# One-hot rows and gate pieces from per-token compares with per-partition scalars, in the gate stage of a PEER layer

## The chip, the core and the metric

The kernel runs on one core of a Trainium2 chip. The metric is the device time of one execution in microseconds (us), taken as the median of several runs. Engines are named as in the profile: PE (TensorE's matmuls) and PEld (its weight loads), DVE (VectorE), ACT (ScalarE), POOL (GpSimd), SP (SyncE, which issues the DMAs here).

## What is computed

One layer of a streaming encoder over 512 prompt tokens and 32 sample tokens (544 in all) with model width 1024: differential attention and retention, cross attention, and then a PEER layer, which is where the change lies. The PEER part of the reference, cut:

```python
q = (hb @ w_pq).reshape(PEER_BLOCK, PEER_HEADS, 2, D_KEY // 2)
s1 = einsum('tpd,pnd->tpn', q[:, :, 0], pk1); s2 = einsum('tpd,pnd->tpn', q[:, :, 1], pk2)
v1, i1 = lax.top_k(s1, 16); v2, i2 = lax.top_k(s2, 16)
cand = v1[..., :, None] + v2[..., None, :]
sc, pos = lax.top_k(cand.reshape(..., 256), 16)
e = take_along_axis(i1[..., :, None] * 128 + i2[..., None, :], pos)
gate = softmax(sc)
act = gelu(einsum('tpkd,td->tpk', u_tab[e], hb))
out = einsum('tpk,tpkd->td', gate * act, v_tab[e])
```

There are 8 heads, 128 keys on each side, 128 x 128 = 16384 experts and 16 chosen experts per head, so each token has 128 chosen (key 1, key 2, gate) triples.

## The kernel before, in words

The kernel gathers nothing. It computes the activation of every expert for every token (128 blocks of `u`, each of 128 experts by 1024, times the 1024 x 544 hidden state), builds a dense gate for every expert and token, multiplies the two, and multiplies the result with all of `v`.

Products in f32 quality are made of three passes with operands split into a high and a low half (`passes`, lines 725 to 730). For each block of `u`, SP loads it into a ring (`weights`, L363), ACT makes the high half (`high`, L1443), POOL makes the low half (`low`, L640: block minus high half, one operation of 128 x 1024 with two inputs in SBUF), PE runs `unit` for the two halves of the tokens (8 chunks x 3 passes x 2 = 48 matmuls of 272 columns, L728 to L730), ACT applies Gelu (L1476) into `actb`, and SP stores it to scratch (L556). Two slots of high and low halves alternate.

The dense gates come from one-hot rows. The 128 chosen triples of a token lie on the 128 partitions: `selT[:, 0]` holds key 1, `selT[:, 1]` key 2, `selT[:, 2]` the gate, each with one column per token. For a token, `hot2` is the row of 128 columns that is 1 where the column number equals key 2; `gated` is the row that holds the gate where the column number equals key 1, and 0 elsewhere. A matmul of the two sums over the 128 triples and gives the token's 128 x 128 gates. To keep f32 quality with bf16 operands, the gate is split into three bf16 `pieces`, so there are three `gated` rows per token and three matmuls into the same output.

The work is grouped by 8 tokens (`TOK8`), 4 such groups (`GROUP`) to a chunk of 32 tokens, 17 chunks (`NCHUNK`): 68 groups in all. Order on each engine in this stage, which is written out by hand:

- PE (L1127 to L1130): for each group one `first_products` unit (48 matmuls, 128 blocks of `u` in all, 68 of them in this stage) and then `gate_products` (L1116 to L1125): wait for `hot_ready`, then 8 tokens x 3 pieces = 24 matmuls of 128 columns in bf16 (L1123) into two banks of 4 tokens each, with `g_ready` raised after each bank. Before the stage PE runs units alone, and after it 8 more units (`U3_GROUPS`), and then the second products with `v`.
- ACT (`gate_chunk`, L1503 to L1514): the next block's high half, two Gelus, and two copies of the gates (L1512) from the banks into `gst`.
- SP: the block loads and activation stores, and once per chunk the store of `gst` (L562).
- POOL: one low half per unit.
- DVE (L1870 to L1890): once, the three pieces of all gates (L1872, L1874); then for each group, after a wait for `g_ready` that lets it run two groups ahead of PE (`hot2` and `gated` have two slots each, `j % 2`): a wide compare that makes `hot1` for 8 tokens (L1885), a semaphore step, a wide compare that makes `hot2` (L1886), and three wide multiplies of `hot1` by a piece (L1888). Each has 8 x 128 = 1024 columns; the per-token values are spread over 128 columns with a step of 0. The last raises `hot_ready`.

DVE has no other work in this stage. `iota` holds 0 to 127 in every partition, in f32.

Of the kernel before, what the change touches and what calls it, by code (L numbers as in the profile page):

```python
# [26 lines left out]
ALU = mybir.AluOpType  # L27
# [4 lines left out]
BF16 = mybir.dt.bfloat16  # L32
U32 = mybir.dt.uint32

P = 128
# [6 lines left out]
NT = len(TILES)  # L42
# [6 lines left out]
KEYS = 128  # L49
# [46 lines left out]
TOK8 = 8  # L96
CTOK = GROUP * TOK8
# [38 lines left out]
def encoder_step(nc, d):  # L136

    with ExitStack() as whole:
# [14 lines left out]
        iota = plan.place("iota", [P, P])  # L153
# [105 lines left out]
        gates_at = first.end  # L259
        gate_plan = Plan(nc, gates_at)  # L260
        hot2 = gate_plan.place("hot2", [P, 2, TOK8, KEYS], BF16)
        hot1 = gate_plan.place("hot1", [P, 2, TOK8, KEYS], BF16)
        gated = gate_plan.place("gated", [P, 2, 3, TOK8, KEYS], BF16)
        pieces = gate_plan.place("pieces", [P, 3, NT * P], BF16)
        selT = gate_plan.place("selT", [P, 3, NT * P])
        gst = gate_plan.place("gst", [P, 2, KEYS, CTOK])
        sel = gate_plan.place("sel", [P, NT, 3, P])
# [1297 lines left out]
        def _(dve):  # L1565
            step = Steps(dve, vec)
# [53 lines left out]
            for m in range(2):  # L1620
                a = dve.tensor_tensor_reduce(out=lam_in[:, 2 * m], in0=lam_in[:, 2 * m], in1=lam_in[:, 2 * m + 1],
                                             scale=1.0, scalar=0.0, op0=ALU.mult, op1=ALU.add,
                                             accum_out=lam[:, m:m + 1])
# [180 lines left out]
            for x in (v16, i16, c16, p16):  # L1804
                a = step.link(dve.memset(x[:], 0))
# [62 lines left out]


            dve.wait_ge(selT_taken, 1)  # L1870
            for q in range(3):
                step.link(dve.tensor_copy(pieces[:, q], selT[:, 2]))  # L1872
                if q < 2:
                    step.link(dve.tensor_tensor(selT[:, 2], selT[:, 2], pieces[:, q], ALU.subtract))  # L1874
            with dve.Fori(0, NCHUNK) as i:
                step.restart()
                for j in range(GROUP):
                    dve.wait_ge(g_ready, (i * GROUP + j) * 2 + 2)
                    tok = bass.ds(i * CTOK + j * TOK8, TOK8)

                    def spread(k):
                        return selT[:, k, tok][:, :, None].to_broadcast([P, TOK8, KEYS])

                    every = iota[:][:, None, :].to_broadcast([P, TOK8, KEYS])
                    step.link(dve.tensor_tensor(hot1[:, j % 2], every, spread(0), ALU.is_equal))  # L1885
                    dve.tensor_tensor(hot2[:, j % 2], every, spread(1), ALU.is_equal)  # L1886
                    for q in range(3):
                        a = dve.tensor_tensor(gated[:, j % 2, q], hot1[:, j % 2],  # L1888
                                              pieces[:, q, tok][:, :, None].to_broadcast([P, TOK8, KEYS]), ALU.mult)
                    a.then_inc(hot_ready, 1)  # L1890


# [136 lines left out]
```

## Time and profile before

| | |
|---|---|
| median of 3 runs | 2628.68 us (2627.41 to 2629.49) |
| span of the profiled execution, first to last instruction | 2627.8 us |
| PE busy in the span | 2351.1 us (89%) |
| DVE busy | 1824.0 us (69%) |
| ACT busy | 868.8 us (33%) |
| POOL busy | 900.5 us (34%) |
| first and last group of gate products on PE start at | 1096.7 and 1635.2 us |
| mean granted TensorE clock, share of full speed | 0.960 |

For the profiled execution the profile gives the span; the runs' own times are from 0.4 us below it to 1.7 us above it, with the median 0.9 us above it. A line of the profile names the source line, the engine, the operation, output and inputs by the program's names, the shape (partitions x columns and type), the number of instructions, busy time and mean time of one, and the idle time of the engine just before them with what ended it. Names are without their numbers, so `hot1` and `hot2` both read `hot`. A tile written without an input shape has input and output of one shape. In the timeline the first two columns are start and duration in us, and neighbouring instructions of one kind are merged into one line with their count.

### The profile page before, as it was taken

Reading aid. Unit: us, or ns where it says so; the run is one execution under the profiler, and the core shown is the slowest. Engines: PE = TensorE matmul, PEld = TensorE weight load, DVE = VectorE, ACT = ScalarE, POOL = GpSimd, SP = SyncE. Lnnn points to the kernel's source line nnn. Section 1 sums busy time; section 2 is a strip of 40 time slices with the busy share of each in tenths; the row PEclk is TensorE's granted clock in tenths of the full one; section 3 lists DMA queues with packets and bytes.
Section 4 is the critical chain, followed back from the end, with each engine's and each line's share of the span. In section 5 each row is a group of like instructions: output and inputs, shape, how many; then the busy total and the mean of one; then the engine's idle time right before and its main releaser. Section 6 shows DMA issues by size and latency. Waiting matters only on the chain.

```text
span 2627.8 us, 49280 instructions
## 1 busy us (share of the span) xinstructions
PE 2351.1 (89%) x18541; PEld 2281.4 (87%) x18541; DVE 1824.0 (69%) x2736; ACT 868.8 (33%) x1375; POOL 900.5 (34%) x352
## 2 busy tenths in 40 slices
PE   5999987887999995999999999999889989998997
PEld 5888877787899995999999999988888888888887
DVE  6344454346888898699999998166666666666665
ACT  4434333232234432344444444322212221222121
POOL 2212232133233342333333333534433433343331
PEclk9999998998999997999999999999999999999998
DMA  4232121211223442344444444664454455444530
GB/s 184 83 101 99 58 78 67 78 48 56 80 95 132 133 135 73 123 164 163 162 162 168 167 166 170 225 213 140 152 166 136 142 155 164 132 148 154 159 98 34
DMA packets 168557, 339.18 MB, mean 129 GB/s; under 512 B 10512, under 2 KB 84400, under 8 KB 166192
## 3 DMA queue, kind: packets, MB, share of 16 engines
q1 hardware_dynamic: 168496, 338.46, 38.7%
q8 instruction: 27, 0.44, 0.1%
q14 instruction: 34, 0.28, 0.0%
HBM read 260.04 MB, written 78.38 MB: 129 GB/s over the span
## 4 chain that ended last, share of the span: by engine, by line
issue 35%; PE 35%; POOL 12%; DVE 11%; ACT 6%; DVEq 0%; POOLq 0%; DMA 0%; ACTq 0%; SPq 0%
POOL u_lo L640 11%; PE bank L728 10%; PE bank L730 9%; PE bank L729 9%; DVE w_lo L1896 6%; ACT v_hi L1525 3%; ACT w_hi L1530 1%; PE bank L790 1%; DVE wf L1907 1%; PE bank L997 1%; DVE mixedT L1599 1%; PE bank L781 1%; PE bank L1025 1%; DVE rmo L1721 1%; DVE xT L1917 1%
## 5 line engine op out<-in xcount | busy, mean ns | idle before, releaser
L728 PE MATMUL bank<-h_hi,u_hi 128*128 128x272 f32 x3136 | 926.0, 295 | 83.0 <-POOL u_lo L640 32.6
L730 PE MATMUL bank<-h_hi,u_lo 128*128 128x272 f32 x3136 | 913.8, 291 | 0.0
L729 PE MATMUL bank<-h_lo,u_hi 128*128 128x272 f32 x3136 | 909.7, 290 | 0.0
L640 POOL TENSOR_TENSOR u_lo<-wring,u_hi 128x1024 fp32r<-128x1024 f32 x196 | 521.8, 2662 | 1067.9 <-ACT u_hi L1443 667.7
L728 PE MATMUL bank<-w_hi,v_hi 128*128 128x272 f32 x2048 | 613.6, 300 | 101.6 <-DVE xT L1917 98.4
L728 PEld LDWEIGHTS bank<-h_hi,u_hi 128*128 128x128 f32 x3136 | 598.6, 191 | 95.8 <-issue 63.3
L729 PE MATMUL bank<-w_lo,v_hi 128*128 128x272 f32 x2048 | 609.7, 298 | 0.0
L730 PE MATMUL bank<-w_hi,v_lo 128*128 128x272 f32 x2048 | 607.9, 297 | 0.0
L729 PEld LDWEIGHTS bank<-h_lo,u_hi 128*128 128x128 f32 x3136 | 598.8, 191 | 0.5
L730 PEld LDWEIGHTS bank<-h_hi,u_lo 128*128 128x128 f32 x3136 | 597.1, 190 | 0.0
L640 POOL TENSOR_TENSOR v_lo<-wring,v_hi 128x1024 fp32r<-128x1024 f32 x128 | 346.8, 2739 | 542.3 <-ACT v_hi L1525 542.3
L728 PEld LDWEIGHTS bank<-w_hi,v_hi 128*128 128x128 f32 x2048 | 407.0, 199 | 108.4 <-DVE xT L1917 105.0
L729 PEld LDWEIGHTS bank<-w_lo,v_hi 128*128 128x128 f32 x2048 | 405.9, 198 | 0.0
L730 PEld LDWEIGHTS bank<-w_hi,v_lo 128*128 128x128 f32 x2048 | 405.5, 198 | 0.0
L1917 DVE TENSOR_TENSOR xT<-bank,xT 128x272 f32<-128x272 f32 x512 | 204.4, 437 | 281.6 <-PE bank L730 281.4
L1888 DVE TENSOR_TENSOR gated<-hot,pieces 128x1024 bf16<-128x1024 bf16 x204 | 377.9, 1907 | 0.0
L1525 ACT ACTIVATE v_hi<-wring 128x1024 fp32r<-128x1024 f32 x128 | 125.4, 1048 | 448.8 <-PE bank L730 437.8
L1896 DVE TENSOR_TENSOR w_lo<-wf,w_hi 128x544 fp32r<-128x544 f32 x128 | 211.4, 1651 | 59.3 <-ACT w_hi L1530 56.4
L1476 ACT ACTIVATE actb<-bank 128x272 f32<-128x272 f32 x256 | 101.9, 399 | 449.8 <-PE bank L730 447.7
L1907 DVE TENSOR_TENSOR wf<-a,g 128x544 f32<-128x544 f32 x128 | 184.5, 1462 | 34.2 <-DMA g<-scratch_gates 29.6
L1530 ACT ACTIVATE w_hi<-wf 128x544 fp32r<-128x544 f32 x128 | 80.3, 650 | 244.1 <-DVE wf L1907 244.1
L1512 ACT ACTIVATE gst<-bank 128x512 f32<-128x512 f32 x136 | 139.5, 1137 | 60.2 <-PE bank L1123 60.2
(223 smaller groups left out, 1988.0 us busy)
## 6 DMA issues: line engine op xcount, KB each, us to landing
wring<-in_u SPq DMA_DIRECT2D x128, 512.0 KB, 3.7
wring<-in_v SPq DMA_DIRECT2D x128, 512.0 KB, 3.3
scratch_act<-actb SPq DMA_DIRECT2D x128, 272.0 KB, 2.1
scratch_gates<-gst SPq DMA_DIRECT2D x17, 2048.0 KB, 7.3
a<-scratch_act SPq DMA_DIRECT2D x32, 1088.0 KB, 7.2
g<-scratch_gates SPq DMA_DIRECT2D x32, 1088.0 KB, 9.9
wring<-in_w_in SPq DMA_DIRECT2D x28, 512.0 KB, 3.8
wring<-in_w_x SPq DMA_DIRECT2D x24, 512.0 KB, 4.1
```

Source lines behind the costliest of these rows:

```text
L640: pool.tensor_tensor(dst, wring[:, slot], hi.bitcast(F32), ALU.subtract).then_inc(lo_ready, 1)
L728: pe.matmul(out, whi, xhi, start=first, stop=False)
L729: pe.matmul(out, whi, xlo, start=False, stop=False)
L730: return pe.matmul(out, wlo, xhi, start=False, stop=last)
L1476: act.activation(actb[:, j, half(h)], bank[(2 * j + h) % 4][:, 0:HT], ACT.Gelu).then_inc(unit_taken, 1)
L1512: act.activation(gst[:, p, :, t0:t0 + 4].rearrange("p k t -> p t k"), bank[4 + b][:].rearrange("p (t k) -> p t k", t=4), ACT.Copy).then_in ...
L1525: act.activation(vs[p][0][:, j].rearrange("p (c n) -> p c n", c=C), wring[:, j], ACT.Copy).then_inc(hi_ready, 1)
L1530: act.activation(wbs[p][0][:, j], wf[:, j % 2], ACT.Copy).then_inc(whi_ready, 1)
L1888: a = dve.tensor_tensor(gated[:, j % 2, q], hot1[:, j % 2], pieces[:, q, tok][:, :, None].to_broadcast([P, TOK8, KEYS]), ALU.mult)
L1896: dve.tensor_tensor(wbs[p][1][:, j], wf[:, j % 2], wbs[p][0][:, j].bitcast(F32), ALU.subtract).then_inc(w_ready, 1)
L1907: dve.tensor_tensor(wf[:, j % 2].rearrange("p (c t) -> p c t", c=NCHUNK), aring[p][:, j].rearrange("p (c t) -> p c t", c=NCHUNK), gring[p] ...
L1917: dve.tensor_tensor(xT[:, b, half(h)], bank[n % 8][:, 0:HT], xT[:, b, half(h)], ALU.add).then_inc(y_taken, 1)
```

## The change

`hot1` goes away. Each token gets four operations of 128 columns: one compare of the key numbers `keys_h` (bf16) with the token's key 2, read from a column of `selT` as a per-partition scalar, and three operations that compare with key 1 and multiply by a piece of the gate, both per-partition scalars. Both scalars of an operation have one type, so `pieces` is now kept in f32: each is rounded to bf16 in `rounded` and cast back. `keys_h` is made once from `iota`. The waits and the semaphore for PE stay as they are; the semaphore step between `hot1` and its readers goes.

```diff
@@ -259,9 +259,10 @@
         hot2 = gate_plan.place("hot2", [P, 2, TOK8, KEYS], BF16)
-        hot1 = gate_plan.place("hot1", [P, 2, TOK8, KEYS], BF16)
+        keys_h = gate_plan.place("keys_h", [P, KEYS], BF16)
         gated = gate_plan.place("gated", [P, 2, 3, TOK8, KEYS], BF16)
-        pieces = gate_plan.place("pieces", [P, 3, NT * P], BF16)
+        rounded = gate_plan.place("rounded", [P, NT * P], BF16)
+        pieces = gate_plan.place("pieces", [P, 3, NT * P])
@@ -1868,25 +1869,22 @@
             dve.wait_ge(selT_taken, 1)
+            step.link(dve.tensor_copy(keys_h[:], iota[:]))
             for q in range(3):
-                step.link(dve.tensor_copy(pieces[:, q], selT[:, 2]))
+                step.link(dve.tensor_copy(rounded[:], selT[:, 2]))
+                step.link(dve.tensor_copy(pieces[:, q], rounded[:]))
                 if q < 2:
                     step.link(dve.tensor_tensor(selT[:, 2], selT[:, 2], pieces[:, q], ALU.subtract))
             with dve.Fori(0, NCHUNK) as i:
                 step.restart()
                 for j in range(GROUP):
                     dve.wait_ge(g_ready, (i * GROUP + j) * 2 + 2)
-                    tok = bass.ds(i * CTOK + j * TOK8, TOK8)
-
-                    def spread(k):
-                        return selT[:, k, tok][:, :, None].to_broadcast([P, TOK8, KEYS])
-
-                    every = iota[:][:, None, :].to_broadcast([P, TOK8, KEYS])
-                    step.link(dve.tensor_tensor(hot1[:, j % 2], every, spread(0), ALU.is_equal))
-                    dve.tensor_tensor(hot2[:, j % 2], every, spread(1), ALU.is_equal)
-                    for q in range(3):
-                        a = dve.tensor_tensor(gated[:, j % 2, q], hot1[:, j % 2],
-                                              pieces[:, q, tok][:, :, None].to_broadcast([P, TOK8, KEYS]), ALU.mult)
+                    for u in range(TOK8):
+                        tok = bass.ds(i * CTOK + (j * TOK8 + u), 1)
+                        dve.tensor_scalar(hot2[:, j % 2, u], keys_h[:], selT[:, 1, tok], None, ALU.is_equal)
+                        for q in range(3):
+                            a = dve.tensor_scalar(gated[:, j % 2, q, u], keys_h[:], selT[:, 0, tok],
+                                                  pieces[:, q, tok], ALU.is_equal, ALU.mult)
                     a.then_inc(hot_ready, 1)
```

## Rows read from the trace of the kernel before

**Rows 1.** The page's part 2: busy tenths and granted clock in 40 slices.
```profile
DVE  6344454346888898699999998166666666666665
...
PEclk9999998998999997999999999999999999999998
```

**Rows 2.** Busy time of a stretch: window, length, then PE, PEld, DVE, ACT, POOL, clock, DMA.
```profile
1200.00:1300.00 100.00, 93.87 (x887) 91.32 (x886) 98.29 (x63) 46.03 (x63) 37.67 (x13) 1.00 0.45 162
```

**Rows 3.** Groups of instructions, 1165 to 1643 us: busy us, mean ns, idle before.
```profile
L1888 DVE TENSOR_TENSOR gated<-hot,pieces 128x1024 bf16<-128x1024 bf16 x174 | 329.8, 1951 | 0.0
...
L640 POOL TENSOR_TENSOR u_lo<-wring,u_hi 128x1024 fp32r<-128x1024 f32 x59 | 177.7, 3012 | 300.0 <-ACT u_hi L1443 300.0
...
L1123 PE MATMUL bank<-gated,hot 128*128 128x128 bf16 x1416 | 89.2, 219 | 30.2 <-DVE gated L1888 30.2
...
L1886 DVE TENSOR_TENSOR hot<-iota,selT 128x1024 bf16<-128x1024 f32 x58 | 71.1, 1225 | 8.3
L1885 DVE TENSOR_TENSOR hot<-iota,selT 128x1024 bf16<-128x1024 f32 x58 | 70.3, 1212 | 0.0
```

**Rows 4.** Timeline of PE: starts of the gate products.
```profile
1096.72 1.51 PE L1123 MATMUL bank<-gated,hot 128*128 128x128 bf16 x24
...
1148.85 1.51 PE L1123 MATMUL bank<-gated,hot 128*128 128x128 bf16 x24
...
1205.49 1.51 PE L1123 MATMUL bank<-gated,hot 128*128 128x128 bf16 x24 [0.51 <-DVE gated L1888]
...
1213.60 1.51 PE L1123 MATMUL bank<-gated,hot 128*128 128x128 bf16 x24 [0.51 <-DVE gated L1888]
...
1635.23 1.51 PE L1123 MATMUL bank<-gated,hot 128*128 128x128 bf16 x24 [0.51 <-DVE gated L1888]
```

**Rows 5.** Timeline of DVE: the third group's first operation; one whole group; the next one's first.
```profile
1098.38 1.23 DVE L1885 TENSOR_TENSOR hot<-iota,selT 128x1024 bf16<-128x1024 f32 x1 [5.42 <-PE bank L1123]
...
1205.29 1.21 DVE L1885 TENSOR_TENSOR hot<-iota,selT 128x1024 bf16<-128x1024 f32 x1
1206.64 1.23 DVE L1886 TENSOR_TENSOR hot<-iota,selT 128x1024 bf16<-128x1024 f32 x1
1207.79 5.68 DVE L1888 TENSOR_TENSOR gated<-hot,pieces 128x1024 bf16<-128x1024 bf16 x3
1213.39 1.21 DVE L1885 TENSOR_TENSOR hot<-iota,selT 128x1024 bf16<-128x1024 f32 x1
```

**Rows 6.** Timeline of POOL.
```profile
1073.44 2.39 POOL L640 TENSOR_TENSOR u_lo<-wring,u_hi 128x1024 fp32r<-128x1024 f32 x1 [1.09 <-ACT u_hi L1443]
...
1209.34 3.04 POOL L640 TENSOR_TENSOR u_lo<-wring,u_hi 128x1024 fp32r<-128x1024 f32 x1 [5.06 <-ACT u_hi L1443]
```

**Rows 7.** DVE groups of one shape each, whole span.
```profile
L1664 DVE TENSOR_SCALAR ri<-ri,lam 128x1 f32<-128x1 f32 x16 | 3.4, 214 | 0.6
...
L1762 DVE TENSOR_SCALAR xn<-xm 128x1 f32<-128x1 f32 x16 | 2.5, 154 | 0.5
...
L1666 DVE TENSOR_SCALAR S<-S,ri 128x512 f32<-128x512 f32 x4 | 1.9, 487 | 0.1
...
L1666 DVE TENSOR_SCALAR S<-S,ri 128x128 f32<-128x128 f32 x4 | 1.1, 287 | 0.1
```

**Rows 8.** Timeline of DVE: eight pointer operations, and short copies between register operations.
```profile
2619.06 5.66 DVE L1581 SCALAR_TENSOR_TENSOR yT<-xT,gains,rms 128x544 f32<-128x544 f32 x8
...
669.01 0.23 DVE L1837 COPY pos<-p 128x80 uint32 x1
669.15 0.23 DVE L1838 CAST key<-i 128x80 uint32 x1
```

**Rows 9.** One source line's instructions: durations min, median, max in ns.
```profile
L1888 DVEq FUSED_REGOPS  x204: 53/53/64, 1078.1 to 1628.6; - x102
```

**Rows 10.** Timeline of DVE: the first gate pieces.
```profile
1068.76 0.49 DVE L1872 CAST pieces<-selT 128x640 bf16<-128x640 f32 x1 [20.39 <-ACT selT L1497]
...
1070.15 2.56 DVE L1872 CAST pieces<-selT 128x640 bf16<-128x640 f32 x1
```

## Prediction

> **What bounds the kernel now.** Read the page's slices first. From the eighteenth to the twenty-fourth slice DVE stands at nine tenths, which it holds for more than one slice nowhere else, with TensorE's clock granted at nine tenths or more [rows 1]; that is the stage in which unit products and gate products alternate, and the only one the change touches. In a stretch of it DVE is busy 98.3 of 100 us, PE 93.9, ACT 46.0, POOL 37.7 [rows 2]. The grouped instructions then say who waits: 59 groups of gate products lie in the window and PE idles 30.2 us ahead of them, ended by the last `gated` product, while DVE's operations have next to no idle time [rows 3]. The timeline gives both paces. Before DVE binds, the gate products start at 1096.72 and, seven intervals later, at 1148.85: 7.45 us apart, PE's own pace with all its work. Later they start at 1205.49 and 1213.60: 8.11 us, with 0.51 us of waiting shown [rows 4]. Of 68 groups 60 are at DVE's pace, from 1096.72 to 1635.23. So the stage can shrink to 67 x 7.45 = 499.2 us from 538.5 us: **39.3 us is all that a faster DVE can give**.
>
> DVE's 8.11 us divide so: the first compare starts at 1205.29, the second at 1206.64, the three multiplies at 1207.79, the next group at 1213.39 [rows 5]. An independent operation starts about 0.08 us before the one ahead ends (1.23 long, 1.15 to the next). Five operations without a stall make 1.35 + 1.15 + 3 x 1.14 = 5.92 us; the other 2.2 us is a stall, one per group, laid on one `gated` product (mean 1951 ns in the groups, three together 5.68 [rows 3, 5]). Its cause stands on POOL: its `u_lo` takes 2.39 us where DVE has almost let go, and 3.04 us here, from 1209.34 to 1212.38 [rows 6], the span of the stretched DVE operation. They take turns for something both read through; POOL comes once per group, before and after.
>
> **The change, part by part.** *Removed:* five operations of 1024 columns, 5.92 us a group. *Added:* 8 tokens x 4 = 32 operations of 128 columns, one with one pointer scalar and three with two. No row shows such an operation, so I build it. A TENSOR_SCALAR with a pointer on 512 columns takes 487 ns, on 128 columns 287 ns: 0.52 ns a column (two columns a cycle, f32) and 220 ns fixed [rows 7]. Eight pointer operations in a row confirm the overlap: 5.66 us, first-to-last spacing 0.70 for one of 0.78 [rows 8]. So spacing is duration less 0.08. In bf16 on both sides I take half that time per column: 33 ns, duration 253, **spacing 173 ns**. Bounds: below, the short copies, which start 0.14 us apart with 42 ns of columns [rows 8], so 0.135; above, one column a cycle as in the wide compares (1.21 us for 1024, [rows 5]), 133 ns instead of 33, so 0.273.
>
> The **second pointer** has no row. One costs 214 - 154 = 60 ns on one column [rows 7]. The second may be fetched right behind the first (0) or after it (60 ns). I take 0, since a fetch of one column that costs 60 ns is nearly all latency, and two latencies can overlap; it is a choice, and the largest unknown: 24 x 60 = 1.44 us a group.
>
> Register operations grow from about one per wide operation, 53 to 64 ns [rows 9], to one or two per small one, on DVE's sequencer. The copies keep 0.14 us apart with one each; two would make some 0.19, 24 times: 5.5 us a group, which the 2.2 us stall lets run ahead. I cost them at nothing (cover: the operations' own spacing); uncovered, 0.02 x 24 = 0.5 us a group.
>
> *POOL's stall* stays at 2.2 us if the small operations use that shared path, and goes if they don't. POOL's own operation gets shorter (it waits for 0.2 us of DVE work, not up to 1.2). The Trainium skill ("SBUF — State Buffer", Who interferes with whom) says that a copy or tensor_scalar in a two-port mode and GpSimd lock each other out for a whole instruction; the trace agrees for the cast that took 0.49 us alone and 2.56 us beside POOL [rows 10].
>
> Sum in DVE's time: 32 x 0.173 + 2.20 = **7.74 us a group** against 8.11. DVE can run only two groups ahead, so its chain starts at the third group, 1098.38 [rows 5], and has 66 groups: 66 x 0.37 = 24.4 us less; the end of the gates moves from 1635.2 to 1610.8, above PE's own floor of 1596.
>
> The Trainium skill ("VectorE: DVE Perf Modes", The TRN2 errata) speaks against the change: a fixed latency per instruction, to be spread over tiles of 512 elements or more. Its table has 58 cycles plus columns over four, an estimate of 94 ns each; by it the group would be 3.0 + 2.2 us and PE would set the pace. The rows here have a dearer fixed part, with the pointer in it.
>
> *Preparation, once:* one cast of `iota`, three casts back to f32 (0.49 us each by the unblocked cast, [rows 10]), at worst two more POOL stalls of 2.1: 2 to 6 us. DVE is idle 5.42 us ahead of the third group [rows 5] and is two groups ahead of PE then, so nothing lands on the path; without that cover, up to 6 us once. The moved buffers add no transfer; SP and POOL issue the same work. What follows the gates (last unit products, then the second products) is PE's and only starts earlier. Next late after DVE is PE; ACT has half its time free, and `u_lo` ends at 1212.38, 2.5 us before its products could start (1213.60 + 1.32), so POOL has room at 7.45 us too.
>
> The span is 2627.8 us, the median of the runs 2628.7: 0.9 us above. 2628.7 - 24.4 = **2604 us**.
>
> **Rivals.**
> *A. PE's floor.* If the small operations come out at 0.16 us or less (the copies say 0.135 to 0.15), DVE needs 32 x 0.16 + 2.2 = 7.3 us and PE's 7.45 us rules: 2628.7 - 39.3 = 2589 us. For: the copies. Against: they have no pointer.
> *B. The second pointer is paid in full (slower).* Place: the 24 two-pointer operations of each group. 8 x 0.173 + 24 x 0.233 + 2.2 = 9.18 us; 66 x 1.07 = 70.6 us more: 2699 us. It decides from (8.11 - 7.74) / 24 = 15 ns per second pointer on. For: one pointer is visibly not hidden. Against: nothing but the overlap argument.
> *C. The faster column rate is not taken*, so the change doesn't do what it says: 32 x 0.273 = 8.74 us. At one column a cycle it reads through one path alone, so the stall goes too; 66 x 0.63: 2670 us. At two columns a cycle (0.207) with the stall it would be 8.82 us, 2676 us. For: no row has bf16 in and out of a TENSOR_SCALAR. Against: the f32 rows reach two columns a cycle with a pointer.
> *D. POOL can't get in between closely following small operations* and waits for all 32: its `u_lo` would end some 3 us later in the period, about at the point where the product needs it; DVE then has no stall, and the pace is about the same 7.7 us. It changes no number, so it shares the forecast's chance.
>
> **How the numbers follow.** Forecast (with D) 0.38, A 0.15, B 0.26, C 0.12; the remaining 0.09 is a second pointer that costs part, around 10 to 20 ns, which lands within a few us of no change on either side. A difference under about 0.2% (5 us) can't be told from none. Faster: 0.38 + 0.15 and a little of the rest, 0.54; same 0.07; slower 0.26 + 0.12 and a little, 0.39. The range goes from just under A to B: 2587 to 2700. Both signs hold much chance; the forecast's own range, with the spacing between 0.16 and 0.18, is 2589 to 2618.
>
> **What would show it.** The gate products' interval: 7.74 us right, 7.45 A, 9.2 B, 8.7 C. The spacing of one-pointer against two-pointer operations: 173 and 173, or 173 and 233. Their duration: 253 ns, or 353 in C. The stall: one small operation in each group stretched by 2.2 us where POOL works; `u_lo` near 2.4 us instead of 3.0. PE's wait for `gated` in most groups, but about 0.2 us instead of 0.5. The forecast is wrong if the gate stage doesn't carry the whole difference.

## The result and the profile after

| | before | after |
|---|---|---|
| median, us | 2629.1 | 2685.2 |
| ratio to before | | 1.0216, interval 1.0202 to 1.0231 |
| span of the profiled execution, us | 2627.8 | 2684.4 |
| first to last group of gate products, us | 538.5 | 586.1 |
| interval of the gate products where DVE binds, us | 8.11 | 8.81 |
| mean granted TensorE clock | 0.960 | 0.958 |

The change makes the kernel **56.1 us slower**; the forecast was 25 us faster. The number lies inside the range, near rival B (2699 us). The spans differ by 56.6 us: 47.6 in the gate stage, 2.0 ahead of its first product (1098.72 against 1096.72) and 7.0 behind it (985.8 us from the start of the last group of gate products to the start of the kernel's last matmul, 978.8 before). The 2.0 us are there before the changed part runs: DVE's first instruction of it starts, with the same idle time ahead of it, at 1070.81, in the kernel before at 1068.76 [rows 10].

```profile
1070.81 0.23 DVE L1872 CAST keys_h<-iota 128x128 bf16<-128x128 f32 x1 [20.38 <-ACT selT L1498]
```

The page's part 2 of the kernel after, in slices of 67 us. The stretch of nines on DVE is longer and fuller than in [rows 1]; the clock is as high as before.

```profile
DVE  5444454347888896999999999266666666566665
...
PEclk9999998899999997999999999999998999999998
```

A window in the middle of the stage, columns as in [rows 2]: DVE is busy all 100 us instead of 98.3, PE falls from 93.9 to 86.6, POOL from 37.7 to 26.8.

```profile
1200.00:1300.00 100.00, 86.57 (x830) 84.23 (x829) 100.00 (x368) 42.88 (x58) 26.82 (x11) 1.00 0.39 138
```

The timeline of PE, for [rows 4]. The first group of gate products waits for nothing. In mid stage they start 8.82 us apart (8.81 is the usual interval, and 64 of 67 are near it; the other three are 7.45), and the wait ahead of them has gone from 0.51 to 1.2 us. 64 x 8.812 + 3 x 7.447 = 586.3 us, the stage.

```profile
1098.72 1.51 PE L1124 MATMUL bank<-gated,hot 128*128 128x128 bf16 x24
...
1199.85 1.51 PE L1124 MATMUL bank<-gated,hot 128*128 128x128 bf16 x24 [1.19 <-DVE gated L1886]
...
1208.67 1.51 PE L1124 MATMUL bank<-gated,hot 128*128 128x128 bf16 x24 [1.22 <-DVE gated L1886]
...
1684.82 1.51 PE L1124 MATMUL bank<-gated,hot 128*128 128x128 bf16 x24 [1.21 <-DVE gated L1886]
```

The timeline of DVE where POOL's turn falls, for [rows 5]. A token without a stall runs from 1202.98 to 1203.81: 0.16 us to the first multiply, 0.67 us for the three of them. The next `hot2` takes 2.39 us instead of 0.24.

```profile
1202.98 0.24 DVE L1884 TENSOR_SCALAR hot<-keys_h,selT 128x128 bf16<-128x128 bf16 x1
1203.14 0.74 DVE L1886 TENSOR_SCALAR gated<-keys_h,selT,pieces 128x128 bf16<-128x128 bf16 x3
1203.81 2.39 DVE L1884 TENSOR_SCALAR hot<-keys_h,selT 128x128 bf16<-128x128 bf16 x1
1206.12 0.75 DVE L1886 TENSOR_SCALAR gated<-keys_h,selT,pieces 128x128 bf16<-128x128 bf16 x3
```

The timeline of POOL, for [rows 6]: its low half begins 0.10 us ahead of that stalled operation and takes 2.44 us instead of 3.04.

```profile
1203.71 2.44 POOL L641 TENSOR_TENSOR u_lo<-wring,u_hi 128x1024 fp32r<-128x1024 f32 x1 [6.38 <-ACT u_hi L1444]
```

The instructions of the two lines, shortest, median and longest in ns, with the register operations of DVE's sequencer. One pointer takes 244 ns, two take 303 (the stalled ones are the longest). Each compare has one register operation of 57 ns; of the gated ones (three to a token) two in three have one, and there is an address operation of 40 ns per token.

```profile
L1884 DVEq FUSED_REGOPS  x544: 57/57/75, 1080.5 to 1679.2; - x182
L1884 DVE TENSOR_SCALAR hot<-keys_h,selT x544: 235/244/2448, 1080.7 to 1683.8; 128x128 bf16<-128x128 bf16 x182
...
L1886 DVE TENSOR_SCALAR gated<-keys_h,selT,pieces x1632: 296/303/2553, 1080.8 to 1684.4; 128x128 bf16<-128x128 bf16 x182
L1886 DVEq FUSED_REGOPS  x1088: 57/57/75, 1080.7 to 1679.8; - x182
L1886 DVEq ALU_OP  x544: 40/40/40, 1080.8 to 1679.6; - x182
```

The groups from 1165 to 1690 us, for [rows 3]. The stall now sits on `hot` (mean 514 ns over operations of 244), and 59 groups of gate products wait 72.0 us in all, 1.22 us each, where it was 0.51.

```profile
L1886 DVE TENSOR_SCALAR gated<-keys_h,selT,pieces 128x128 bf16<-128x128 bf16 x1415 | 353.7, 303 | 0.0
...
L1884 DVE TENSOR_SCALAR hot<-keys_h,selT 128x128 bf16<-128x128 bf16 x471 | 241.9, 514 | 0.0
...
L1124 PE MATMUL bank<-gated,hot 128*128 128x128 bf16 x1436 | 90.4, 219 | 72.0 <-DVE gated L1886 72.0
```

The spacings are 0.163 us behind a compare and 0.223 us behind a gated operation. So DVE's group is 8 x 0.163 + 24 x 0.223 = 6.66 us of operations, against 5.92 before, and 8.81 less that leaves 2.15 us for POOL's stall, against 2.2. The small operations alone lose 0.74 us a group, and the stall gives back almost nothing of it.

### The profile page after: what moved, and what is told of

Read it like the earlier page. It is cut to its first block, busy times and chain, and to the rows that moved or that the text cites. A ratio compares the mean times of both kernels' runs of the same rounds, so it can differ in the third digit from the quotient of the medians.

```text
span 2684.4 us, 52956 instructions
## 1 busy us (share of the span) xinstructions
PE 2358.4 (88%) x18541; PEld 2287.6 (85%) x18541; DVE 1887.2 (70%) x4576; ACT 867.9 (32%) x1375; POOL 861.3 (32%) x352
## 4 chain that ended last, share of the span: by engine, by line
issue 37%; PE 35%; POOL 11%; DVE 11%; ACT 6%; DVEq 0%; POOLq 0%; DMA 0%; ACTq 0%; SPq 0%
POOL u_lo L641 10%; PE bank L729 10%; PE bank L731 9%; PE bank L730 9%; DVE w_lo L1894 6%; ACT v_hi L1526 3%; ACT w_hi L1531 1%; PE bank L791 1%; DVE wf L1905 1%; DVE mixedT L1600 1%; PE bank L998 1%; PE bank L782 1%; PE bank L1026 1%; DVE rmo L1722 1%; DVE xT L1915 1%
## 5 line engine op out<-in xcount | busy, mean ns | idle before, releaser
L641 POOL TENSOR_TENSOR u_lo<-wring,u_hi 128x1024 fp32r<-128x1024 f32 x196 | 481.0, 2454 | 1157.7 <-ACT u_hi L1444 756.1
L1886 DVE TENSOR_SCALAR gated<-keys_h,selT,pieces 128x128 bf16<-128x128 bf16 x1632 | 420.9, 311 | 0.0
L1884 DVE TENSOR_SCALAR hot<-keys_h,selT 128x128 bf16<-128x128 bf16 x544 | 270.4, 497 | 0.5 <-DVE pieces L1875 0.5
```

Source lines behind the costliest of these rows:

```text
L641: pool.tensor_tensor(dst, wring[:, slot], hi.bitcast(F32), ALU.subtract).then_inc(lo_ready, 1)
L1884: dve.tensor_scalar(hot2[:, j % 2, u], keys_h[:], selT[:, 1, tok], None, ALU.is_equal)
L1886: a = dve.tensor_scalar(gated[:, j % 2, q, u], keys_h[:], selT[:, 0, tok], pieces[:, q, tok], ALU.is_equal, ALU.mult)
```

## The experiments

**The second pointer by itself.** In the gated operation the second scalar becomes a constant; its length in columns, its output and POOL's work stay. The gates are then made without their values (each is the same constant), so the PEER outputs are not the reference's.

```diff
-                            pieces[:, q, tok], ALU.is_equal, ALU.mult)
+                            0.0625, ALU.is_equal, ALU.mult)
```

> The 24 gated operations of a group keep their compare, their multiply and their first pointer scalar; the second scalar is the constant 0.0625 (so the gates are not the reference's). If each pointer scalar is fetched after the one before it (about 59 ns each, from 303 against 244 ns in the changed kernel), the gated operations fall to 244 ns and 0.165 us apart, the group to 32 x 0.165 + 2.14 = 7.4 us, and PE's own 7.45 us rules: 67 x 7.45 = 499 us of gate stage against 586, about 2598 us in all. If the second arithmetic step costs the 59 ns, nothing changes: 8.81 us a group, 2685 us.

Measured: 2600.3 us, 0.9888 of before (0.9872 to 0.9905). The stage takes 498.9 us and the gate products start 7.45 us apart. The source line of the gated operation, then the timeline of one token and the two ahead of and behind it:

```profile
L1886 DVE TENSOR_SCALAR gated<-keys_h,selT x1632: 235/246/2490, 1079.5 to 1590.3; 128x128 bf16<-128x128 bf16 x182
```

```profile
1201.98 0.24 DVE L1884 TENSOR_SCALAR hot<-keys_h,selT 128x128 bf16<-128x128 bf16 x1
1202.14 0.57 DVE L1886 TENSOR_SCALAR gated<-keys_h,selT 128x128 bf16<-128x128 bf16 x3
1202.63 0.24 DVE L1884 TENSOR_SCALAR hot<-keys_h,selT 128x128 bf16<-128x128 bf16 x1
```

With one pointer a gated operation takes the compare's 246 ns, and a token takes 0.65 us instead of 0.83. The group's sum is 8 x 0.65 + 2.2 = 7.4 us, at PE's pace, and PE shows no wait for DVE any more. **The second pointer costs 59 ns of an operation's duration and 60 of the spacing (0.223 against 0.163), and it alone turns the change from a gain of 29 us to a loss of 56.**

**DVE's sequencer.** Another way to 59 ns more per operation is the register work that the moving token index brings, which e1 lessens too. Here both pointers stay and the index is fixed, so that no register operations are left in the loop; every chunk of tokens then takes the first chunk's keys and gates, so the gates are not the reference's.

```diff
-                        tok = bass.ds(i * CTOK + (j * TOK8 + u), 1)
+                        tok = slice(j * TOK8 + u, j * TOK8 + u + 1)
```

> All pointer scalars of the changed kernel point to columns that are fixed per group of the loop body, so no register arithmetic stands ahead of any operation (the gates are those of the first 32 tokens again and again, so not the reference's). If the sequencer's register operations set the pace, the 32 operations come closer together and the group falls well under 8.81 us (towards 7.45). If the pointer fetch in the operation sets it, durations stay 244 and 303 ns, the group stays at 8.81 us and the time at 2685 us.

Measured: 2688.1 us, 1.0222 (1.0205 to 1.0239); interval 8.81, operations of 246 and 305 ns. Nothing is gained, so the register work is hidden and the 59 ns go with the second pointer scalar in the operation itself.

**The column rate.** `iota` is read in f32 in place of its bf16 copy, in both operations (the compare's edit is shown, the gated operation has the same).

```diff
-                        dve.tensor_scalar(hot2[:, j % 2, u], keys_h[:], selT[:, 1, tok], None, ALU.is_equal)
+                        dve.tensor_scalar(hot2[:, j % 2, u], iota[:], selT[:, 1, tok], None, ALU.is_equal)
```

> The 32 operations read the f32 iota in place of the bf16 keys_h. If the changed kernel's operations take four columns a cycle and these take two, each gets 33 ns longer (277 and 336 ns), the group goes to 8.81 + 1.07 = 9.9 us and the time to about 2685 + 66 x 1.07 = 2756 us. If the bf16 operations did not take the fastest rate, nothing changes: 2685 us.

Measured: 2761.9 us, 1.0509 (1.0491 to 1.0526); interval 9.92. Timeline of DVE, one token:

```profile
1200.57 0.28 DVE L1884 TENSOR_SCALAR hot<-iota,selT 128x128 bf16<-128x128 f32 x1
1200.77 0.84 DVE L1886 TENSOR_SCALAR gated<-iota,selT,pieces 128x128 bf16<-128x128 f32 x3
```

The medians are 275 and 336 ns, 31 and 33 more. At two columns a cycle 128 columns take 67 ns ([rows 7]), at four 33: the difference is what going from the one to the other gives, so the changed kernel does run at the faster rate. Rival C, with 353 ns an operation, is out by the 244 ns already. 32 x 0.033 = 1.06 us of the 1.11 us a group are accounted for.

**Where the buffers lie.** The change also moves the stage's buffers, which could be behind the 7 us at the end. The kernel before with a gap of 1280 bytes ahead of `selT`, which puts `selT` and what lies behind it where the change puts them (`gated` and `pieces` stay):

```diff
+        gate_plan.place("gap", [P, 640], BF16)
```

> The kernel before with 1280 bytes left free ahead of selT, so that the buffers behind lie where the change puts them; no instruction differs. The changed kernel is 7 us slower also behind the gate stage. If the moved buffers cause that, this one is at about 2629 + 7 = 2636 us. If they don't, it is at 2629 us.

Measured: 2629.4 us, 1.0000 (0.9991 to 1.0010), 978.6 us from the start of the last group of gate products on. Moving these buffers does nothing.

**A version that keeps the wide operations and takes the bf16 rate.** Two tokens lie innermost (pair, column, token of the pair), keys and index are copied to bf16 once, so every operand of the five wide operations is bf16 and advances by neighbouring elements; PE reads its operands at every second element.

```diff
-        hot2 = gate_plan.place("hot2", [P, 2, TOK8, KEYS], BF16)
+        hot2 = gate_plan.place("hot2", [P, 2, TOK8 // R, KEYS, R], BF16)
...
+        keys_r = gate_plan.place("keys_r", [P, KEYS, R], BF16)
+        keys_t = gate_plan.place("keys_t", [P, 2, T], BF16)
...
-                            m = pe.matmul(bank[4 + b][:, k * P:(k + 1) * P], hot2[:, j % 2, 4 * b + k],
-                                          gated[:, j % 2, q, 4 * b + k], start=q == 0, stop=q == 2)
+                            r, o = (4 * b + k) // R, (4 * b + k) % R
+                            m = pe.matmul(bank[4 + b][:, k * P:(k + 1) * P], hot2[:, j % 2, r, :, o],
+                                          gated[:, j % 2, q, r, :, o], start=q == 0, stop=q == 2)
...
-                        return selT[:, k, tok][:, :, None].to_broadcast([P, TOK8, KEYS])
+                        return x.rearrange("p (a r) -> p a r", r=R)[:, :, None, :].to_broadcast(whole)
```

> From the kernel before: the five wide operations of a group are kept, but all operands are bf16 and the tokens lie in pairs innermost (4 pairs x 128 columns x 2 tokens), so that no operand repeats one element along the innermost dimension. PE reads its gate operands with a step of 2 elements. If the wide compare and multiply then take two columns a cycle: 0.61 us apart, 5 x 0.61 + 0.15 + 2.2 = 5.4 us a group, PE's 7.45 us rules and the time is about 2629 - 39 = 2590 us. If they stay at one column a cycle, 2629 us or a little more. If PE reads strided operands at half the rate, the gate products take 1.3 us more per group: 8.8 us, about 2675 us.

Measured with R = 2: **2592.2 us, 0.9862 (0.9845 to 0.9878)**, the fastest of all that ran, and it beats both kernels. Groups of its stage (1165 to 1560 us):

```profile
L1895 DVE TENSOR_TENSOR gated<-hot,pieces 128x1024 bf16<-128x1024 bf16 x159 | 216.3, 1415 | 0.0
...
L1893 DVE TENSOR_TENSOR hot<-keys_r,keys_t 128x1024 bf16<-128x1024 bf16 x53 | 36.7, 692 | 7.5
L1892 DVE TENSOR_TENSOR hot<-keys_r,keys_t 128x1024 bf16<-128x1024 bf16 x53 | 36.7, 692 | 103.8 <-PE bank L1127 103.8
```

A wide compare takes 692 ns instead of 1212, without a pointer. The multiplies, whose operands are bf16 in both kernels, go from a median of 1219 ns to 685; the longest, 3420 and 2884, hold the stall, which is still on one of the three. The source lines of the multiplies, the kernel before first:

```profile
L1888 DVE TENSOR_TENSOR gated<-hot,pieces x204: 1208/1219/3420, 1079.2 to 1631.7; 128x1024 bf16<-128x1024 bf16 x102
```

```profile
L1895 DVE TENSOR_TENSOR gated<-hot,pieces x204: 682/685/2884, 1078.4 to 1586.5; 128x1024 bf16<-128x1024 bf16 x102
```

DVE now waits for PE, 1.96 us a group. The Trainium skill ("VectorE: DVE Perf Modes", What auto-detection actually checks) says that an operation with two tensor inputs gets its doubled rate where every tensor is 16-bit with a step of one element; the trace agrees: 1219 ns for a multiply with the values spread at step 0 along the innermost dimension, 685 with pairs there. PE has become the bound, as its timeline shows with no wait ahead of the gate products:

```profile
1200.47 1.55 PE L1127 MATMUL bank<-gated,hot 128*128 128x128 bf16 x24
1207.95 1.55 PE L1127 MATMUL bank<-gated,hot 128*128 128x128 bf16 x24
```

7.48 us apart, 0.03 above the floor of 7.45, which is about what the gate products grew by (1.55 for 1.51).

**All eight tokens innermost.** The same with R = 8: fewer dimensions for DVE, and PE reads at every eighth element, 16 bytes apart.

> As v1_pairs with all eight tokens innermost (128 columns x 8 tokens), so PE reads with a step of 8 elements (16 bytes). If the rate of the wide operations depends only on two neighbouring elements, it is as v1_pairs on DVE; if PE's reading depends on the step, it shows here and not there: gate products above 1.5 us a group. 2590 us if neither costs.

Measured: 3012.5 us, 1.1465 (1.1445 to 1.1484). DVE's operations are the same 692 ns. Group and timeline of PE:

```profile
L1127 PE MATMUL bank<-gated,hot 128*128 128x128 bf16 x694 | 168.2, 415 | 0.0
```

```profile
1203.98 5.81 PE L1127 MATMUL bank<-gated,hot 128*128 128x128 bf16 x24
```

The 24 gate products take 5.81 us instead of 1.51, and each group 13.65 us. That is more than the 4.3 us that they grew by (7.45 + 4.3 = 11.8). The remaining 1.9 us are the clock's. The mean granted clock of the stage falls to 0.76, where v1 has 1.00 in the same window:

```profile
1200.00:1300.00 100.00, 100.00 (x538) 85.38 (x537) 39.31 (x37) 27.63 (x37) 17.72 (x8) 0.76 0.28 96
```

PE is busy all 100 us here; the level falls to 1.2 GHz during the slow gate products and rises some 4.5 us after them. The unit products ahead of a group and behind it show the two levels:

```profile
1203.72 0.29 PE L732 MATMUL bank<-h_lo,u_hi 128*128 128x272 f32 x1
1203.85 0.29 PE L733 MATMUL bank<-h_hi,u_lo 128*128 128x272 f32 x1
...
1209.81 0.43 PE L732 MATMUL bank<-h_lo,u_hi 128*128 128x272 f32 x1
1210.04 0.43 PE L733 MATMUL bank<-h_hi,u_lo 128*128 128x272 f32 x1
```

Some 19 unit products behind each group start 0.23 us apart instead of 0.125, which makes 2.0 us. The gate products themselves are 0.23 us apart at either level, so their slowness is not the clock's. The Trainium skill ("SBUF — State Buffer", Specifications (TRN2)) gives lines of 16 bytes and asks for two hits in each for full bandwidth: a step of 16 bytes has one hit per line, a step of 4 bytes has four, and 5.81 against 1.55 us goes with that. Both operands of the matmul have the step; no run tells which of them costs the time.

**The 7 us behind the stage.** They came with `after` (985.8 us from the start of the last group of gate products to the start of the last matmul), e1 (989.7), e2 (989.2) and e3 (988.5), and not with e4 (978.6) or v1 (978.9), whose DVE program is about as short as the kernel's before. Since the matter might be the length of the program, the kernel before gets 100 fills of one column on DVE, run once ahead of the gate loop:

```diff
+            for k in range(100):
+                dve.memset(lam_in[:, k // DK, k % DK:k % DK + 1], 0.0)
```

> The kernel before with 100 one-column fills of unused scratch on DVE ahead of the gate loop, where DVE is idle (6 us of work under 5.4 us of idle time, so 0 to 2 us on the path). Behind the gate stage the changed kernel and all its relatives show 0.72 us from the last add to the first product at DVE's loop branch, the kernel before 0.61, and 7 to 11 us more from the last gate product to the end. If the length or the place of DVE's program makes that, this kernel shows 0.72 us too and 7 to 11 us more behind the stage: about 2637 us. If it is something in the small operations themselves, the 0.61 us and the 2629 us (plus 0 to 2) stay.

Measured: 2641.7 us, 1.0045 (1.0028 to 1.0062); the stage is unchanged (538.5 us, 8.11), and 990.5 us lie behind it. So instructions that take no part in the second products slow them, 11.7 us here. A part of it is seen at DVE's loop branch, the step from the last `xT` addition of one turn to the first `wf` product of the next. Before, after and e5, timelines of DVE (1st and 2nd row of each):

```profile
2122.97 0.44 DVE L1917 TENSOR_TENSOR xT<-bank,xT 128x272 f32<-128x272 f32 x1 [1.06 <-PE bank L730]
2123.58 3.57 DVE L1907 TENSOR_TENSOR wf<-a,g 128x544 f32<-128x544 f32 x2 [0.17 <-issue]
```

```profile
2116.36 0.44 DVE L1915 TENSOR_TENSOR xT<-bank,xT 128x272 f32<-128x272 f32 x1 [1.06 <-PE bank L731]
2117.09 3.58 DVE L1905 TENSOR_TENSOR wf<-a,g 128x544 f32<-128x544 f32 x2 [0.28 <-issue]
```

```profile
2128.93 0.44 DVE L1919 TENSOR_TENSOR xT<-bank,xT 128x272 f32<-128x272 f32 x1 [1.06 <-PE bank L730]
2129.68 3.57 DVE L1909 TENSOR_TENSOR wf<-a,g 128x544 f32<-128x544 f32 x2 [0.31 <-issue]
```

0.61 us before, 0.73 after, 0.75 in e5, and PE waits as much longer at every second turn (3.34, 3.45 and 3.47 us). Over PE's 33 waits behind the stage this sums to no more than 1.5 us (105.7 to 107.2 us, before and after). The rest is PE's own time. Windows over the second products, before and after:

```profile
1690.00:2627.00 937.00, 823.35 (x6148) 816.04 (x6148) 599.52 (x777) 203.95 (x260) 337.76 (x125) 0.94 0.46 146
```

```profile
1740.00:2684.00 944.00, 828.89 (x6148) 821.53 (x6148) 601.07 (x777) 204.01 (x260) 338.98 (x124) 0.93 0.46 144
```

The same 6148 matmuls take 5.5 us more, at a mean granted clock of 0.93 instead of 0.94, and 5.5 + 1.5 are the 7.0 us. The stretches at the lower level, 1.2 GHz, which come behind PE's waits, add up to 119.9 us before, 133.6 after and 145.8 in e5: before, all but the last are of one length, and after, five are twice as long. That the longer step at the branch brings this about is only argued, but it fits every profile: the six with a step of 0.72 to 0.75 us (after, e1, e2, e3, e5 and e6 below) have 985.8 to 990.5 us behind the stage, and those with 0.61 (before, e4, v1 and e7 below) 978.6 to 980.6. (v2 has 0.61 too; its last group is itself 4 us longer, so its figure doesn't compare.)

**Small operations for `hot2` alone.** The kernel before with its wide compare for `hot2` replaced by eight operations with one pointer; the rest stays wide. `keys_h` is made as in the changed kernel (not shown).

```diff
-                    dve.tensor_tensor(hot2[:, j % 2], every, spread(1), ALU.is_equal)
+                    for u in range(TOK8):
+                        dve.tensor_scalar(hot2[:, j % 2, u], keys_h[:], selT[:, 1, bass.ds(i * CTOK + (j * TOK8 + u), 1)],
+                                          None, ALU.is_equal)
```

> One part of the change alone: hot2 is made by eight one-pointer operations of 128 columns, hot1 and the three multiplies stay wide. Eight at 0.165 us are 1.32 us in place of 1.15, so the group takes 8.11 + 0.17 = 8.28 us and the stage 66 x 0.17 = 11 us more: 2640 us, or up to 10 us above that if the later part gets slower as in the changed kernel. If the loss were only in the sequencer or in the waits of small operations as such, the group would grow by a quarter of the change's 0.70 us or more.

Measured: 2633.5 us, 1.0017 (1.0007 to 1.0026). The stage came out otherwise than expected: 7.95 us a group, not 8.28, and faster than before; the 9 us won there are lost again behind it (987.7 us). Timelines of DVE and of POOL:

```profile
1201.28 3.48 DVE L1892 TENSOR_TENSOR gated<-hot,pieces 128x1024 bf16<-128x1024 bf16 x3
1204.68 1.22 DVE L1887 TENSOR_TENSOR hot<-iota,selT 128x1024 bf16<-128x1024 f32 x1
1206.05 3.27 DVE L1889 TENSOR_SCALAR hot<-keys_h,selT 128x128 bf16<-128x128 bf16 x8
1209.23 1.21 DVE L1892 TENSOR_TENSOR gated<-hot,pieces 128x1024 bf16<-128x1024 bf16 x1
```

```profile
1202.28 5.84 POOL L641 TENSOR_TENSOR u_lo<-wring,u_hi 128x1024 fp32r<-128x1024 f32 x1 [2.11 <-ACT u_hi L1444]
```

This is rival D's picture, with the roles turned. POOL's low half, ready to start at 1202.28, doesn't get in among the wide operations, and finishes at 1208.12, 2.07 us after the small ones have begun. Those take 3.18 us where eight of 0.163 would take 1.30, so the stall is 1.88 us here instead of 2.2. The waits of the stage (1160 to 1600 us) show who is late for PE now, POOL rather than DVE, which has next to no idle time either:

```profile
POOL u_lo L641 <- ACT u_hi L1444: 119.4, 56, 2.5
...
PE bank L729 <- POOL u_lo L641: 19.0, 56, 0.4
```

Why POOL got in among three wide multiplies before, after a wait of 0.65 us ([rows 6]: 3.04 less 2.39), and not here, stays open. The one-pointer operations are no gain for `hot2`: 1.30 us for eight against 1.15 for the wide one. The stage is faster by the shorter stall: 8.11 + 0.15 - 0.3 is 7.96.

**A later start of the second products.** 16 small matmuls behind the last gates put PE off by 3.5 us, to see if the phase alone brings the 7 us.

```diff
+            for k in range(16):
+                pe.matmul(bank[6][:, 0:P], ones[:], ident[:], start=True, stop=True)
```

> The kernel before with 16 f32 products of 128 columns into an idle bank on PE behind the last gate products: some 3 us, so that the second products start about 3 us later. If the part behind them only moves, the time is about 2632 us. If the phase between the second products' groups and the stretches at half clock decides what it costs, as between the kernel before (978.8 us from the last gate product to the last matmul) and the changed one (985.8), the rest changes by several us more than the delay, in either direction.

Measured: 2633.1 us, 1.0015 (1.0005 to 1.0024), 980.6 us behind the stage in the profiled execution; the branch step stays at 0.61 us. The second products begin 3.5 us later and end only 1.8 us later, so when they begin has some effect, but here it takes time away and doesn't bring the 7 us. The ten runs lie between 2629.4 and 2638.5 us, a wider spread than the kernel before has (2624.5 to 2631.1), so that other phases cost nothing is not shown.

What is shown, by e5, is that the length or place of DVE's program has a price here. Through what is open. Loading instructions again in each turn is not seen: between 1800 and 2600 us the trace has no packet on a queue for instructions, in the kernel before or in e5, while e5's longer step comes back at every second turn.

## Why the prediction was wrong

- **What bounds the stage: right.** DVE sets the pace through one wait per group. PE's floor of 7.45 us a group and 499.2 us for the stage was met by e1 with 7.45 and 498.9.
- **The one-pointer operation: nearly right.** Spacing 173 ns forecast, 163 measured; 253 ns long forecast, 244 measured. The half column time for bf16 (33 ns) was confirmed by e3. The 10 ns are worth 32 x 0.010 = 0.32 us a group. (The lower bound of 0.135 is 0.131 by the prediction's own figures, 0.14 - 0.042 + 0.033.)
- **The second pointer: the step that failed.** "I take 0, since ... two latencies can overlap." They don't: 303 against 244 ns in the same kernel, and e1 takes those 59 ns away with the pointer. That is the same price as the first (60 ns, [rows 7]) and the upper of the two bounds. 24 x 0.060 = 1.44 us a group in the spacing, where 15 ns each were enough to turn the sign. The argument for 0 rested on no row, and the row that there was priced one pointer visibly.
- **POOL's stall: right.** 2.2 us forecast, 2.15 measured, on one small operation, and POOL's own operation at 2.43 us, as foreseen (2.4). Rival D didn't come about in the changed kernel.
- **The register operations: right at nothing** (e2). Their sum was set too high: by its own figures 24 x 0.19 + 8 x 0.14 is 5.7 us a group, not 5.5, and the trace has 3 x 57 + 40 = 211 ns a token, 1.7 us a group.
- **The sum.** 7.74 + 1.44 - 0.32 - 0.05 = 8.81 us, as measured. Without the second pointer it would have been 7.37, so that even a right zero would have led to rival A's floor rather than to the forecast's 7.74.
- **Rival B** had the mechanism and the sign. Its 9.18 us were too high by the 10 ns of spacing and the 0.05 of the stall. That its 2699 us came within 14 us of the measured time is in part luck: 0.37 us a group too much made some 24 us, and the 2.0 and 7.0 us outside the stage, which it didn't foresee, offset nine of them.
- **The checks named.** PE's wait, forecast to shrink to about 0.2 us, grew to 1.22. "The forecast is wrong if the gate stage doesn't carry the whole difference": it carries 47.6 of 56.6 us. That what follows the gates only moves was the second step that failed, by 7.0 us; that the preparation is free held: the first gate products start 2.0 us later, but so does DVE's first instruction of the changed part, ahead of the preparation. What made these 2.0 us is open; the start of the stage differs by some 1 us between kernels with the same preparation (1095.9 in e7, 1096.7 before; 1097.4 in e3, 1098.7 after).
- **The fixed cost by the Trainium skill** ("VectorE: DVE Perf Modes", The TRN2 errata). Its table gave an estimate of 94 ns per operation; measured spacings are 163 and 223 ns. The rows of the kernel before were the better guide.

## What to carry to other kernels

Price a per-partition scalar read through a pointer like an operand of its own: here each cost about 60 ns, the second as much as the first, which for 128 columns of bf16 is nearly twice the column work. Before wide operations with spread values are cut into small ones, see if the spread can be laid out with pairs innermost in bf16: that took the wide operations from 1219 to 685 ns and took the stage to PE's floor, as long as the matmul's reading step stayed small. And where a cost has a row for one and none for two, take the row twice unless a row speaks against it.

## What the runs showed that was not expected

- A matmul operand in bf16 read with a step of 4 bytes costs almost nothing (1.55 us for 24 against 1.51), with a step of 16 bytes 5.81 us, and behind those the granted clock is at the lower level, which costs another 1.9 us a group.
- 100 one-column fills in DVE's program, run once and long before, made the second products 11.7 us slower at the end of the kernel. A change that lengthens an engine's program can have a price in a later stage that it doesn't touch.
- DVE and POOL take turns, but where POOL gets in depends on what DVE runs: after 0.65 us of waiting among wide operations before, at once among small ones after, and in e6 only as the wide ones ended, after some 3.4 us (5.84 less 2.39).
